# A float32 conv mixer ahead of an MLP on one core: tap pacing, places of small products, diagonals, and one-row modulation products

## The reference, cut to what matters

```python
mod = silu(c) @ mod_w + mod_b                     # (1, 6*2048)
sh1, sc1, g1, sh2, sc2, g2 = split(mod, 6)
h = rms_norm(x, norm1_g) * (1 + sc1) + sh1
u = h @ w_in + b_in                               # 2048 -> 4096
a, gt = split(u, 2); u = a * sigmoid(gt)
u = depthwise_conv(u, dw_w, 31 taps, causal) + dw_b
u = silu(layer_norm(u, ln_g, ln_b))
x = x + (1 + g1) * (u @ w_out + b_out)
h = rms_norm(x, norm2_g) * (1 + sc2) + sh2        # then the MLP, then the second block
```

## Time and profile before

| what | us |
|---|---|
| median of 3 runs | 2834.72 |
| profiled execution, its own time | 2834.11 |
| its span | 2832.3 |
| TensorE busy in the span | 2606.8 (92%) |
| VectorE / ScalarE / GpSimd busy | 1680.9 / 1153.9 / 621.7 |
| mean granted TensorE clock | 0.954 of full |

### The profile page before, as it was taken

One profiled execution on the slowest core, in us unless ns is written; L12 is line 12 of the kernel. 1 busy time (PEld: TensorE's weight loads), 2 busy tenths in 40 slices (PEclk: granted clock), 3 DMA queues, 4 the chain that ended last, 5 costly groups with the idle time before them and its releaser, 6 DMA issues. The chain is left out here.

```text
span 2832.3 us, 29855 instructions
## 1 busy us (share of the span) xinstructions
PE 2606.8 (92%) x11022; PEld 2049.3 (72%) x11022; DVE 1680.9 (59%) x1996; ACT 1153.9 (41%) x1470; POOL 621.7 (22%) x277
## 2 busy tenths in 40 slices
PE   4777878898999999999898999998989999999998
PEld 2343437776888888888677778876868888888886
DVE  5665472667687776777765233279467655455555
ACT  2033422544434434344444445443444434443443
POOL 1034633321222222222132334443400000000000
PEclk9889888698999999999999999999989999999999
DMA  9965653665888888898863555688568866666664
GB/s 312 381 227 171 224 165 123 211 210 201 291 300 294 286 309 295 292 310 289 255 168 115 154 152 170 194 284 305 182 203 276 283 189 190 193 186 193 191 189 141
DMA packets 340160, 644.69 MB, mean 228 GB/s; under 512 B 30000, under 2 KB 63440, under 8 KB 338992
## 3 DMA queue, kind: packets, MB, share of 16 engines
q1 hardware_dynamic: 338752, 642.09, 69.8%
q0 software_dynamic: 448, 0.43, 0.1%
q10 hardware_dynamic: 816, 0.26, 0.0%
HBM read 640.60 MB, written 2.10 MB: 227 GB/s over the span
## 5 line engine op out<-in xcount | busy, mean ns | idle before, releaser
L82 ACT ACTIVATE whi<-stage 128x1024 fp32r<-128x1024 f32 x752 | 795.4, 1059 | 1034.3 <-PE bank L82 894.0
L82 DVE TENSOR_TENSOR wlo<-stage,whi 128x1024 fp32r<-128x1024 f32 x588 | 750.6, 1277 | 775.0 <-ACT whi L82 754.1
L82 PE MATMUL bank<-whi,hhi 128*128 128x512 f32 x2016 | 809.7, 402 | 34.3 <-DVE wlo L82 9.8
L82 PE MATMUL bank<-wlo,hhi 128*128 128x512 f32 x2016 | 793.5, 394 | 0.0
L82 PE MATMUL bank<-whi,hlo 128*128 128x512 f32 x2016 | 793.2, 393 | 0.0
L82 POOL TENSOR_TENSOR wlo<-stage,whi 128x1024 fp32r<-128x1024 f32 x164 | 413.0, 2519 | 1061.6 <-ACT whi L82 984.6
L82 PEld LDWEIGHTS bank<-whi,hhi 128*128 128x128 f32 x2016 | 384.6, 191 | 124.5 <-ACT scr L82 18.6
L82 PEld LDWEIGHTS bank<-whi,hlo 128*128 128x128 f32 x2016 | 383.6, 190 | 82.3
L82 PEld LDWEIGHTS bank<-wlo,hhi 128*128 128x128 f32 x2016 | 384.4, 191 | 80.9 <-issue 3.1
L82 PE MATMUL bank<-whi,uhi 128*128 128x512 f32 x992 | 390.9, 394 | 0.0
L82 PE MATMUL bank<-whi,ulo 128*128 128x512 f32 x992 | 389.8, 393 | 0.0
(11 more groups left out here) (120 smaller groups left out, 1337.7 us busy)
## 6 DMA issues: line engine op xcount, KB each, us to landing
stage<-in_mlp_w SPq DMA_DIRECT2D x256, 512.0 KB, 5.5
stage<-in_mod_w SPq DMA_DIRECT2D x192, 512.0 KB, 6.0
stage<-in_w_ada SPq DMA_DIRECT2D x192, 512.0 KB, 5.4
stage<-in_w_in SPq DMA_DIRECT2D x136, 512.0 KB, 4.1
stage<-in_w_ffn_gate SPq DMA_DIRECT2D x88, 512.0 KB, 4.4
stage<-in_w_ffn_up SPq DMA_DIRECT2D x88, 512.0 KB, 4.4
stage<-in_w_ffn_down SPq DMA_DIRECT2D x88, 512.0 KB, 4.0
stage<-in_conv_w_in SPq DMA_DIRECT2D x128, 256.0 KB, 6.6
```

What stands on the lines that cost most here:

```text
L82: made = fn(*args, **kw)
```

## The change

1. `TAPS_A_TILE` 9 to 5.
2. Channel tile 8 goes from TensorE to DVE: DVE jobs are now (0,1), (2,4), (5,6), (7,8), (9,10), (11,12), (13), (15); TensorE keeps 3 and 14.
3. The diagonals of ct 3 are made ahead too, into `G` (during the first two modulation quarters); those of ct 14 two quarters later. The PE job of ct 3 is queued two tiles later (`L_PE_JOB`), in 4 parts of 8 taps.
4. `G` is therefore free only after ct 3: the loads of the gate biases wait for `conv_done[3]`, and they and the load of conv_b_out go from ahead of tile 80 to ahead of tile 126 of the stream.
5. 66, 4 and 10 modulation tiles in conv-in, tail and conv-out, where there were 60, 8 and 12; the pair set (0,1,0) goes ahead of the gates.
6. Places: the partition sums of aside sets come 3 tiles after the last product (`L_SUMS`), the squares of the layer norm 2 after the centring (`L_SQUARE`).
7. `mod_on_pe`: one column of `CS` is the stationary operand and the tile the moving one: two products of 512 columns into one row of two banks, accumulated over the 16 tiles. `mod_end` copies the two rows to `scr` on ACT, and two tiles later 8 products turn them into columns.

```diff
-N_MOD_IN = 60
-N_MOD_TAIL = 8
+N_MOD_IN = 66
+N_MOD_TAIL = 4
 N_MOD_OUT = 14
-TAPS_A_TILE = 9
+TAPS_A_TILE = 5
+L_PE_JOB = 2
+L_SQUARE = 2
+L_SUMS = 3
-DVE_JOBS = ((0, 1), (2, 4), (5, 6), (7, 9), (10, 11), (12,), (13,), (15,))
-PE_JOBS = (3, 8, 14)
+DVE_JOBS = ((0, 1), (2, 4), (5, 6), (7, 8), (9, 10), (11, 12), (13,), (15,))
+PE_JOBS = (3, 14)
...
-                        later(2 if m["aside"] else 1, lambda m=m: mod_end(m))
+                        later(L_SUMS if m["aside"] else 1, lambda m=m: mod_end(m))
... mod_on_pe
-            for j in range(8):
-                m["last"] = T.put(nc.tensor.matmul, bank[:, j * NKT + kt:j * NKT + kt + 1], w[:, j * 128:(j + 1) * 128],
-                                  c, start=True, stop=True, signal=(j == 7), after=[landed, m["cond"]] + m["free"])
+            for j in range(2):
+                m["last"] = T.put(nc.tensor.matmul, groups[m["group"]][j][0:1, :], c, w[:, j * 512:(j + 1) * 512],
+                                  start=(kt == 0), stop=(kt == NKT - 1), signal=(j == 1),
+                                  after=[landed, m["cond"]] + m["free"])
... mod_end
-                group_free[m["group"]] = [mod_columns(m, groups[m["group"]][0], m["last"])]
+                    row[j] = (i, buf, A.put(nc.scalar.activation, buf[0:1, :], groups[m["group"]][j][0:1, :], ACT.Copy,
+                                            after=[m["last"]] + free))
+                group_free[m["group"]] = [row[0][2], row[1][2]]
+                def columns():
+                    b, bank, free = misc.take()
+                    for j in range(8):
+                        _, buf, made = row[j // 4]
+                        t = T.put(nc.tensor.matmul, bank[:, j:j + 1], buf[0:1, (j % 4) * 128:(j % 4) * 128 + 128],
+                                  ones[0:1, 0:1], start=True, stop=True, after=[made, consts] + free)
...
+                later(2, columns)
...
+        diag_store = {PE_JOBS[0]: G[:, :, :].rearrange("p a (b n) -> p (a b) n", n=S), PE_JOBS[1]: hx[:, NKT:, :]}
...
-                            if ct in PE_JOBS:
+                            if ct == PE_JOBS[1]:
                                 pe_job(ct)
+                            elif ct in PE_JOBS:
+                                later(L_PE_JOB, lambda ct=ct: pe_job(ct))
...
-                    ln_square(two, ln["squares"][1], ln["squares"][2], n == 0, False, t)
+                    later(L_SQUARE, lambda: ln_square(two, t))
...
-            if q < 2:
-                tasks.append(lambda: diags_ahead(16 * q, min(16 * q + 16, TAPS)))
+            if q > 1:
+                tasks.append(lambda: diags_ahead(PE_JOBS[1], 16 * (q - 2), min(16 * q - 16, TAPS)))
+            else:
+                tasks.append(lambda: diags_ahead(PE_JOBS[0], 16 * q, min(16 * q + 16, TAPS)))
...
-            gate_bias_load(0, 2, [])
-            gate_bias_load(0, 5, [])
+            gate_bias_load(0, 2, [conv_done[PE_JOBS[0]]])
+            gate_bias_load(0, 5, [conv_done[PE_JOBS[0]]])
...
-        beside[80] = load_gates
+        beside[126] = load_gates
```

More of the change, by code:

```diff
@@ L28 @@
 L_PROJ = 6
-N_MOD_IN = 60
-N_MOD_TAIL = 8
+N_MOD_IN = 66
+N_MOD_TAIL = 4
 N_MOD_OUT = 14
-TAPS_A_TILE = 9
-DVE_JOBS = ((0, 1), (2, 4), (5, 6), (7, 9), (10, 11), (12,), (13,), (15,))
-PE_JOBS = (3, 8, 14)
-PE_LAST = 14
+TAPS_A_TILE = 5
[4 more added lines that the diff above has]
+PE_JOBS = (3, 14)
 LN_LATE = (13, 14, 15)
@@ L405, in mod_on_pe @@
                 group_free[m["group"]] = None
-            bank = groups[m["group"]][0]
-            for j in range(8):
-                m["last"] = T.put(nc.tensor.matmul, bank[:, j * NKT + kt:j * NKT + kt + 1], w[:, j * 128:(j + 1) * 128],
-                                  c, start=True, stop=True, signal=(j == 7), after=[landed, m["cond"]] + m["free"])
+            for j in range(2):
+                m["last"] = T.put(nc.tensor.matmul, groups[m["group"]][j][0:1, :], c, w[:, j * 512:(j + 1) * 512],
+                                  start=(kt == 0), stop=(kt == NKT - 1), signal=(j == 1),
+                                  after=[landed, m["cond"]] + m["free"])
             return m["last"]
@@ L419, in mod_columns @@
             columns = [params["A"], params["B"], params["C"]]
[L420 to L429, removed]
+            mod_cols[(n, 0, q)] = V.put(nc.vector.tensor_tensor, sh, bank[:, 0:4], bias[0], ALU.add,
+                                        after=[t] + columns)
+            t1 = V.put(nc.vector.tensor_tensor, sc, bank[:, 4:8], bias[1], ALU.add, after=[t] + columns)
             mod_cols[(n, 1, q)] = V.put(nc.vector.scalar_tensor_tensor, out=sc, in0=sc, scalar=1.0,
@@ L436, in mod_end @@
             if m["aside"] == "PE":
-                group_free[m["group"]] = [mod_columns(m, groups[m["group"]][0], m["last"])]
+                row = []
+                for j in range(2):
+                    row.append(tiles.take())
+                    i, buf, free = row[j]
+                    row[j] = (i, buf, A.put(nc.scalar.activation, buf[0:1, :], groups[m["group"]][j][0:1, :], ACT.Copy,
[7 more added lines that the diff above has]
+                                  ones[0:1, 0:1], start=True, stop=True, after=[made, consts] + free)
+                    for i, _, _ in row:
+                        tiles.give(i, t)
+                    misc.give(b, mod_columns(m, bank, t))
+                later(2, columns)
                 return
@@ L779, in build_program, with diag_of, diags_ahead, pe_job @@
         diags = {}
-        def diag_of(j):
-            return hx[:, NKT + j // 2, 128 * (j % 2):128 * (j % 2) + 128]
-        def diags_ahead(lo, hi_):
+        diag_store = {PE_JOBS[0]: G[:, :, :].rearrange("p a (b n) -> p (a b) n", n=S), PE_JOBS[1]: hx[:, NKT:, :]}
+        def diag_of(ct, j):
+            return diag_store[ct][:, j // 2, 128 * (j % 2):128 * (j % 2) + 128]
+        def diags_ahead(ct, lo, hi_):
             for j in range(lo, hi_):
-                diags[j] = A.put(nc.scalar.activation, diag_of(j), ident[:, :], ACT.Copy, scale=tap(PE_LAST, j),
-                                 after=[consts] + [params[k] for k in tap_params])
-        def pe_job_ahead(ct):
+                diags[ct, j] = A.put(nc.scalar.activation, diag_of(ct, j), ident[:, :], ACT.Copy, scale=tap(ct, j),
+                                     after=[consts] + [params[k] for k in tap_params])
+        def pe_job(ct):
             job = {}
@@ L797, in part @@
                 for j in range(lo, hi_):
-                    t = T.put(nc.tensor.matmul, bank[:, 0:S], diag_of(j), U[:, ct, j:j + S], start=(j == 0),
-                              stop=(j == TAPS - 1), after=[diags[j], u_ready[ct]] + free)
+                    t = T.put(nc.tensor.matmul, bank[:, 0:S], diag_of(ct, j), U[:, ct, j:j + S], start=(j == 0),
+                              stop=(j == TAPS - 1), after=[diags[ct, j], u_ready[ct]] + free)
                 if hi_ == TAPS:
@@ L806, in pe_job_ahead @@
                 pe_taps.append(lambda lo=lo: part(lo, min(lo + 8, TAPS)))
[L808 to L833, removed]
         waiting_jobs = deque(DVE_JOBS)
@@ L903, in build_program, with ln_square @@
         s_ready = {}
-        def ln_square(n, bank, free, first, last, t):
+        def ln_square(n, t):
+            bank, free = ln["squares"][1:]
+            count = ln["n_squares"] = ln.get("n_squares", 0) + 1
+            first, last = count == 1, count == ln["of_squares"]
             i, buf, free_t = tiles.take()
@@ L914, in ln_square @@
             tiles.give(i, t)
-            return t
+            ln["spread"] = t
         def ln_provisional(cts):
@@ L930, in ln_provisional, with centre @@
             groups_of = [cts[k:k + 2] for k in range(0, len(cts), 2)]
-            for n, two in enumerate(groups_of):
-                def centre(n=n, two=two):
+            ln["of_squares"] = len(groups_of) + len(LN_LATE)
+            for two in groups_of:
+                def centre(two=two):
                     w = len(two)
@@ L956, in ln_late @@
                                 stop=last, after=[t, consts] + ln["sums"][2])
-            ln["spread"] = ln_square([ct], ln["squares"][1], ln["squares"][2], False, last, t)
+            ln_square([ct], t)
         def layer_norm():
@@ L1000, in finish @@
                                                       buf.rearrange("p (k n) -> p k n", k=2), [e],
-                                                      [conv_in_read[0], conv_done[PE_LAST]])
+                                                      [conv_in_read[0], conv_done[PE_JOBS[1]]])
                 tiles.give(i, s_ready[ct][1])
@@ L1063, in build_program @@
             rest += ci[p]
-        mods = []
+        mods = mod_pairs(0, 1, 0, aside=True)
         for half in range(2):
             mods += gate_tiles(0, 2, half, aside=True, then=lambda half=half: tasks.append(lambda: add_output_bias(half)))
-        for q in range(3):
+        for q in range(1, 3):
             mods += mod_pairs(0, 1, q, aside=True)
```

## The result

The changed kernel takes 2721.3 us (median of 4 runs, 2719.97 to 2721.85) where the kernel before took 2834.32 in the same job (4 runs): ratio 0.9603, interval 0.9587 to 0.962. That is 113 us less, 4.0%; 2714 with a range of 2692 to 2768 was forecast. The profiled execution has a span of 2719.7 us and a granted clock of 0.975.

The account below looks back on a forecast made before the run. Loads pace 40 to 154.6 us; then engines wait in turn, ScalarE's copies behind VectorE's tap chains. Conv-out's first product at 407.5 instead of 528.5 saves 121 us, conv-out 0: 2834.1 - 121 = 2713, 2714 against the median; range 2692 to 2768.

Parts of the forecast that it names:

- the forecast's 407.5: Conv-out's first product: forecast restart at 407.5 us against 528.5 in the kernel before, 121 us earlier.
- Loads ahead of tile 80: Before r0: moving 3 MB of loads to tile 126 starts r0 7.6 us earlier, bounds 0 and 9.
- The conv stage: r0 to r45: five steps a tile shorten waits; r45 ends at 334 us instead of 442.5.
- the rounds of 31 us: Conv stage after r13: loop from u through taps, copy, evacuation and transposes takes 31 us, against 28.3 of TensorE.
- The small places: Later places remove waits of 12.50 us (TensorE) and 25.62 us (VectorE), part of the 84; diagonals ahead cost 0.
- The tail: r45's end to last modulation tile: 57 us of TensorE work plus 7 of waits, 64 us, ending at 398.
- the first rival: Tail: one-row modulation products keep the clock at its lower level, 27.5 us more, 2741 us; chance 0.15.
- plus 7 of small waits: Tail: 7 us allowed for TensorE's waits, from its 6.5 us idle between 443.7 and 471.8 in the kernel before.
- Conv-out: Conv-out: fewer GpSimd adds against eight more one-row products, taken as 0, bounds -5 and +3 us.
- half clock in the tail: Tail: one-row products use one array column, so the clock stays low; 27.5 us more, 2741 us; chance 0.15.
- the hold on the loads: Tile 126: the wait for conv_done[3] holds the weight stream, making the kernel slower; chance 0.04.
- Stalls stay by half: Conv stage: half the stalls remain, r45 at 369, 35 us more, 2749 us; chance 0.17, with half clock 0.06.

Follow-up runs that it names:

- after: The changed kernel with all seven parts of the change, against the kernel before: 2721.3 us, ratio 0.9603.

## Why the prediction was right

The forecast was 7 us short of the measured median, and 8.4 for the profiled execution, by terms that went both ways (they differ by 8.8; 0.4 is rounding in the forecast's 407.5):

| term | forecast | measured |
|---|---|---|
| r0's start | 142.1 | 139.6 |
| r0 to r45's end | 192 | 191.3 |
| r45's end to the last modulation tile | 64 | 81.2 |
| from there to conv-out's first product | 9 | 11.8 |
| conv-out and after, against before | 0 (-5 to 3) | -8.0 |

That the total came this near is in part luck: the tail took 17 us more than forecast, and 8 us came back in conv-out and behind it, where the sum had 0.

**Loads ahead of tile 80.** Right in place, too small: 10 us for 7.6 (9 us in time when done alone). The forecast took VectorE's wait in front of the last two tiles as the whole price. But VectorE is through the last tile 9.5 us earlier (135.5 for 145.0), near the forecast's upper bound of 9 from the bytes, and the partition sum behind it takes 2.95 us instead of 3.58; ahead of it TensorE had stood idle for 1.75 us, before for 7.52.

**The conv stage.** The step that carried the forecast held: 5 steps against 9 is worth 54 us alone and 71 within the change, ct 8 is worth 14, and the rounds of 31 us were measured as 31.0, 32.1 and 32.1. That the loop runs through ScalarE's copy is shown by the run that took it out. The 71 us are 82 at r45's end, of which 15 come back in the tail. TensorE's idle time is 4 us of 191 where under 15 were asked for, and the clock is 0.98. The wait for `conv_done[3]` costs nothing that shows: the loads moved to tile 126 are issued at 206.63 with no gap ahead of them. (In the sum, "8 taps" at 1.73 us are 8 instructions, two for each tap; it counts instructions, so it stands.)

**The small places.** Wrong in reason: the waits of 12.50 and 25.62 us went for the most part with the backlog. With five steps and the old places they are 5.04 and 6.43 us (the run with five steps in the kernel before), and with nine steps and the later places TensorE still waits 10.06 us for GpSimd at 347.65. The later places measure nothing by themselves. The diagonals made ahead were not tried alone: the run with channel tile 8 on VectorE in the kernel before still makes those of ct 3 between the products, and what lies between it (2765), less the gate loads (9) and the one-row products (12), and after (2721) is some 22 us, which these, the split of the modulation tiles and the places share. How the 22 us divide stays open beyond the places' nought.

**The tail.** This is the term that was mis-sized: 81.2 us for 64. The duration of a tile was right (1.73 us at clock 1.00, not the half clock of the first rival). One reason given for that rival was misread, though: one-column products do not always show 0.53, since the single tile at 463.23 in the earlier trace rows takes 1.84 us. What failed is "plus 7 of small waits": TensorE was idle for 14.7 us. Its busy time was 66.6 us and not 57. Some 3.6 of these 9.6 are the partition sum at 344.05, which the forecast had counted in the conv stage; of the rest, the rows between 348 and 363 at or near half pace make up some 5, with the granted clock at 0.59 from 337 to 360 us, behind the wait of 7.50.

The forecast had GpSimd through with the stage at 316, and it is through at 344.0:

```profile
303.93 4.87 POOL L84 TENSOR_TENSOR R<-R 128x1024 f32<-128x1024 f32 x2 [6.63 <-ACT R L84]
...
316.37 27.63 POOL L84 TENSOR_TENSOR R<-R 128x1024 f32<-128x1024 f32 x11
```

It stood 6.63 us while ScalarE waited for a tap chain (10.94 us, to 302.16), and the second output bias, 7.6 us ahead of 316.37, falls in the last round. So the sum asked for whether GpSimd keeps up in all, and not where it stands when the tail begins. VectorE holds 6.2 us there by another way, which the forecast did not have at all: its 27 us of work were taken to run beside TensorE's, but the transposes for u of ct 14 wait for a bank behind half of it.

**Conv-out.** The bound of -5 was reached (109.7 us earlier at its end than before, against 104.6 at its start), and 3 us more came after it. No run here explains either part.

Of the rivals, half clock in the tail and the hold on the loads did not happen. "Stalls stay by half" happened in the tail only.

## What to carry to other kernels

Where one engine's list holds a copy that waits for a long chain on another, queue the chain's steps at the pace of the other work, so that little stands behind the waiting copy: here that alone was half of the gain. After such a stall is gone, look for waits that lie on each other: taking away one of 7 us brought the next instruction only 3 us forward. Time won at one mark counts only if the next mark moves; and work that needs nothing of the tiles in front of it, as the layer norm here, is worth more early than those tiles are.

## What the runs showed of the hardware

A product with one stationary column and 512 moving ones runs at the full granted clock: 1.00 from 382 to 412 us, 4 instructions in 1.73 us. The same product with 128 stationary columns and one moving, 12 or 15 tiles on end, keeps TensorE busy as well (42.5 of 43 us) and is granted 0.53 to 0.56: 3.3 to 3.4 us for 16 pairs of load and product. A single such tile among other work takes 1.84 us (at 463.23).

The time of such a pair follows the clock: 16 take 1.71 us from start to start at full clock (208.94 to 210.65 in after) and 3.41 us in the series from 394.7 us on of the run with the old products, whose granted clock is 0.50 from 388 to 436 us. The Trainium skill ("TensorE: Matmul & The Clock Gate", "LDWEIGHTS") has one figure for a weight load, columns over 1.2 GHz, which gives an estimate of 1.7 us for the 16 loads. The trace agrees with it at full clock and has twice that at the lower one.
